# A routed-expert stage on one core: straight code per expert, transposes among the down products, up products as three rounded products

## The chip, the cores and the metric

The kernel runs on one core of one Trainium2 chip. The metric is the device time of one execution in microseconds. Three runs of the kernel before took 1823.43, 1825.82 and 1828.92 us; the median is 1825.82 us.

## The reference, cut to what matters

One inference step of a two-layer decoder trunk: 512 prompt tokens and 8 sample tokens, so T = 520 columns of D = 1024 channels, float32. Each layer has a mixer part and a feed-forward part; layer 0's is dense, layer 1's has eight routed experts of which each token uses two. Only the latter changes:

```python
def swiglu(h, w1, w3, w2):
    return (jax.nn.silu(h @ w1) * (h @ w3)) @ w2

def moe_swiglu(h, w_router, b_router, w1, w3, w2):
    logits = h @ w_router + b_router
    top_v, top_i = lax.top_k(logits, TOP_K)          # 2 of 8
    gates = jax.nn.softmax(top_v, axis=-1)
    comb = jnp.sum(one_hot(top_i, 8) * gates[..., None], axis=-2)
    y = jnp.zeros_like(h)
    for e in range(8):
        y = y + comb[..., e:e + 1] * swiglu(h, w1[e], w3[e], w2[e])   # 1024 -> 1408 -> 1024
    return y
```

## The kernel before, in words

All five engines run programs written out by hand and ordered by semaphores; nothing reorders them. After the router, GpSimd scatters each token's row of h to two places in a table in memory, `h_by_expert` (L695), so that the rows of an expert lie together. The counts of the eight experts sum to 1040. They are known only at run time: each engine reads them from the tile `count` (`tokens_of`, L325).

Then TensorE runs a loop over the eight experts (L1080 to L1087). For an expert with at most NW = 256 tokens (all eight here):

- `narrow_rows` (L981): two tiles of 128 rows from `stage` are transposed, 16 transposes of 128 by 128 (L988), into PSUM, and copied by VectorE (L1660) and ScalarE (L1308) into `hn`.
- `narrow_products` (L991), first loop, the **up products**: for each of ET = 11 blocks f of 128 hidden channels, w1 and w3 by `hn`, KD = 8 products of 128 by 128 by n each (L1006), 11 x 2 x 8 = 176 for one expert. They are plain float32 products, and the profile shows each as two pairs of a weight load (LDWEIGHTS) and a MATMUL, 352 pairs. ScalarE takes the Silu (L1313), VectorE the product (L1666) into `Gn`.
- its second loop, the **down products**: 8 blocks q of 11 products of w2 by `Gn` (L1019), 88 for one expert, plain float32, 176 pairs in the profile. ScalarE copies each block out (L1316); behind block q the two transposes of block q - 1 (L1028) turn it back to token rows, which VectorE copies (L1671) and SP's queue writes to `y_by_expert` (L501).

The number of columns n is a constant of the code, so there is one body of code for each of ten widths (`WIDTHS`: 128, 136, 144, 152, 160, 176, 192, 208, 224, 256). `narrow_by_width` (L1071) picks the body by nested comparisons, one for each width (L1076):

```python
                with pe.If(c <= widths[0]):
                    narrow_products(e, widths[0])
                with pe.Else():
                    narrow_by_width(e, c, widths[1:])
```

The forms of the matmuls show the widths that this input takes: expert 0 to 7 run at 128, 136, 128, 144, 136, 208, 152, 128 columns. For more than 256 tokens there is a body `wide`, not run here. SP's queue loads the weights in twelve chunks an expert into a ring of six slots (L525 waits for a slot), each chunk free again when the products that read it are done.

Elsewhere the kernel computes products in another form, which the change takes up. In layer 0's dense part and in both mixers a product of float32 tiles is made of three products of tiles of the rounded type float32r: the upper part of each operand is made by a rounding copy on ScalarE (L1132, L1148), the lower part by a subtraction on GpSimd or VectorE (L604, L1381), and TensorE sums upper by upper, upper by lower and lower by upper (L747 at 260 columns with weights 128 columns wide; L792 at 256 columns has only two of them, with a stationary tile 18 columns wide). In the profile each of these is one pair.

Of the kernel before, what the change touches and what calls it, by code (L numbers as in the profile page):

```python
# [38 lines left out]
AT = [0, 128, 256, 384, T - P]  # L49
PICKS = 2 * T  # L50
ROOM = PICKS + T
NW = 2 * P
WIDTHS = [128, 136, 144, 152, 160, 176, 192, 208, 224, NW]
# [46 lines left out]
def trunk_program(nc, A, O):  # L100
    ctx = ExitStack()
    with ctx:
# [93 lines left out]
        countf = sb("countf", [P, NE])  # L196
        count = sb("count", [P, NE], I32)
# [20 lines left out]
        hexp = cut(big, 11 * T, KD, T)  # L218
        hact = cut(big, 19 * T, 2, T)

        Gn = cut(big, 0, ET, NW)
        hn = cut(big, 11 * T, KD, NW)
        hactn = cut(big, 19 * T, 2, NW)
# [9 lines left out]
        lgT = stat2[0:NE]  # L233

# [62 lines left out]
        def norm_step(tag, k, n):  # L297
# [5 lines left out]
                                          "zero", "h_tr", "h_row", "in_tr", "in_ev", "in_ev1",  # L303
                                          "f_done", "f_act", "f_free", "y_done", "y_free", "yt_tr", "yt_ev",
                                          "y_out", "count", "exp_d", "diag", "g_mm", "g_ev", "x_tr", "x_ev",
                                          "ya", "ss", "ssr", "rr", "scaled", "mods", "const"]}
        Rout = [sem(f"moe_rows_out{t}") for t in range(NT)]
        Rwide = [sem(f"moe_wide_in{t}") for t in range(2, NT)]
# [21 lines left out]

        w_in_v = [A["w_in"][l].rearrange("(k p) (b n) -> b p k n", p=P, n=256) for l in range(DEPTH)]
# [6 lines left out]
        def expert_chunk(e, j):  # L338

            if j < 8:  # L340
                w = A["w1_moe" if j % 2 == 0 else "w3_moe"][0]
                n = P * min(3, ET - 3 * (j // 2))
                return w[e].rearrange("(k p) n -> p k n", p=P)[:, :, (j // 2) * 384:(j // 2) * 384 + n], KD, n
            return A["w2_moe"][0][e].rearrange("(k p) n -> p k n", p=P)[:, :, (j - 8) * 256:(j - 7) * 256], ET, 256

# [46 lines left out]
        def _(sp):  # L392
# [81 lines left out]
            def first_rows(row):  # L474
# [4 lines left out]
            def rest_of_rows(e):  # L479
                c, row = tokens_of(sp, e), first_of(sp, e)  # L480
                with sp.If(c <= NW):
                    for t in range(2, NT):
                        sp.sem_inc(Rwide[t - 2], 16)
                with sp.Else():
                    for t in range(2, NT):
                        free = sp.snap(sp.to_reg(NT * e + t - 1))
                        sp.wait_ge(const_ready, 1)
                        sp.wait_ge(R["in_tr"], free)
                        sp.dma_start(stage[:, t % 2, :], Hd[bass.ds(row + AT[t], P), :]).then_inc(Rwide[t - 2], 16)

            def rows_out(e):


                c, row = tokens_of(sp, e), first_of(sp, e)
                with sp.If(c <= NW):
                    sp.sem_inc(R["y_out"], 16 * (NT - 2))
                    for t in range(2):
                        there = sp.snap(sp.to_reg(NT * e + NT + t))
                        sp.wait_ge(const_ready, 1)
                        sp.wait_ge(R["yt_ev"], there)  # L500
                        sp.dma_start(Yd[bass.ds(row + P * t, P), :], yrow[:, t, :]).then_inc(R["y_out"], 16)  # L501
                with sp.Else():
                    for t in range(NT):
                        there = sp.snap(sp.to_reg(NT * e + t + 2))
                        sp.wait_ge(const_ready, 1)
                        sp.wait_ge(R["yt_ev"], there)
                        sp.dma_start(Yd[bass.ds(row + AT[t], P), :], stage[:, 2, :]).then_inc(R["y_out"], 16)

            sp.wait_ge(R["count"], 2)
            row0 = first_of(sp, 0)  # L510
            for t in range(NT):
                sp.wait_ge(Rout[t], 32)
            first_rows(row0)
            with sp.Fori(0, NE - 1) as e:
                rest_of_rows(e)
                row = first_of(sp, e + 1)
                free = sp.snap(sp.to_reg(NT * e + NT))
                sp.wait_ge(const_ready, 1)
                sp.wait_ge(R["in_tr"], free)
                first_rows(row)  # L520
                for j in range(PER_E):
                    which, n = used(e, j)
                    n = sp.snap(sp.to_reg(n))
                    sp.wait_ge(const_ready, 1)
                    sp.wait_ge(which, n)  # L525
                    j += EXPERT_RING
                    eload(j, expert_chunk(e, j) if j < PER_E else expert_chunk(e + 1, j - PER_E))
                rows_out(e)
            last = sp.snap(sp.to_reg(NE - 1))
            rest_of_rows(last)  # L530
            for j in range(PER_E - EXPERT_RING):
                sp.wait_ge(*used(NE - 1, j))
                eload(j + EXPERT_RING, expert_chunk(NE - 1, j + EXPERT_RING))
            rows_out(last)
# [18 lines left out]
        def _(pool):  # L553
# [67 lines left out]
            for l in range(DEPTH):  # L621
# [53 lines left out]
                if l == 0:  # L675
# [5 lines left out]
                    link(pool.memset(stage[0:T // 5, 2, :], 0.0))  # L681
                    pool.dma_start(Hd[PICKS:ROOM].rearrange("(a p) n -> p a n", a=5),
                                   stage[0:T // 5, 2:3, :].to_broadcast([T // 5, 5, D])).then_inc(R["zero"], 16)
# [1053 lines left out]
```

## Time and profile before

| what | us |
|---|---|
| median of the three runs | 1825.82 |
| span of the profiled execution, first to last instruction | 1826.2 |
| start of the first row transposes of expert 0 | 1076.21 |
| last transposes of expert 7 end | about 1783.2 |
| the stretch of the experts between these | 707.0 |
| TensorE matmuls busy in the whole span | 1479.6 |

The page gives no time of the profiled execution other than its span. An engine's busy time is the union of its instructions' durations. A MATMUL's duration (275 ns and more) is its latency, of which most overlaps its neighbours; how fast matmuls follow each other is read from the chain of waits, where a run of xN matmuls stands with the time in which it passed. "issue" is time in which an engine waited for nothing that the profile shows; the sequencer's own rows (here PEldq) say what it did in it.

### The profile page before, as it was taken

Reading aid. Unit: us, or ns where it says so; the run is one execution under the profiler, and the core shown is the slowest. Engines: PE = TensorE matmul, PEld = TensorE weight load, DVE = VectorE, ACT = ScalarE, POOL = GpSimd, SP = SyncE. Lnnn points to the kernel's source line nnn. Section 1 sums busy time; section 2 is a strip of 40 time slices with the busy share of each in tenths; the row PEclk is TensorE's granted clock in tenths of the full one; section 3 lists DMA queues with packets and bytes.
Section 4 is the critical chain, followed back from the end, with each engine's and each line's share of the span. In section 5 each row is a group of like instructions: output and inputs, shape, how many; then the busy total and the mean of one; then the engine's idle time right before and its main releaser. Section 6 shows DMA issues by size and latency. Waiting matters only on the chain.

```text
span 1826.2 us, 27269 instructions
## 1 busy us (share of the span) xinstructions
PE 1479.6 (81%) x11320; PEld 1411.8 (77%) x11321; DVE 602.4 (33%) x815; ACT 480.2 (26%) x662; POOL 397.8 (22%) x288
## 2 busy tenths in 40 slices
PE   5776877789999999989588859879796919949792
PEld 4555876679999999979577649869796919949692
DVE  6667697623112011146965320101101000000115
ACT  6677312422221122223133221111111100011114
POOL 1102560534434343434524020000000000000004
PEclk9998898899999999989899979889898959979896
DMA  9999121024333322322210469686685833637554
GB/s 321 300 337 316 48 91 46 28 70 120 93 87 98 105 93 56 96 93 70 69 47 6 164 218 306 209 295 210 241 269 183 300 109 110 216 104 234 173 171 163
DMA packets 249862, 286.02 MB, mean 157 GB/s; under 512 B 7589, under 2 KB 241719, under 8 KB 249686
## 3 DMA queue, kind: packets, MB, share of 16 engines
q1 hardware_dynamic: 244886, 272.17, 45.9%
q0 software_dynamic: 3632, 11.08, 1.8%
q8 instruction: 126, 2.06, 0.5%
q10 hardware_dynamic: 1200, 0.56, 0.1%
q14 instruction: 18, 0.15, 0.0%
HBM read 266.45 MB, written 18.05 MB: 156 GB/s over the span
## 4 chain that ended last, share of the span: by engine, by line
PE 66%; DVE 15%; issue 9%; DMA 5%; SPq 2%; ACT 1%; POOL 1%; POOLq 0%; ACTq 0%; DVEq 0%
PE PP L747 28%; PE PP L1006 20%; PE PP L1019 10%; DVE work L1477 7%; DMA mem<-in_w_ada 4%; PE PP L760 2%; DVE stat L1573 1%; PE PP L988 1%; PE PP L792 1%; PE PP L721 1%; PE PP L732 1%; SPq L424 1%; PE PP L1028 1%; DVE stat L1406 1%; DVE mem L1419 1%
## 5 line engine op out<-in xcount | busy, mean ns | idle before, releaser
L747 PE MATMUL PP<-hT_r,mem_r 128*128 128x260 f32 x2624 | 428.5, 284 | 4.6 <-DVE xT L1431 3.2
L1006 PE MATMUL PP<-big,mem 128*128 128x128 f32 (+4 forms) x2816 | 362.4, 293 | 49.5 <-issue 49.2
L1006 PEld LDWEIGHTS PP<-big,mem 128*128 128x128 f32 x2816 | 360.6, 195 | 52.1 <-issue 49.6
L604 POOL TENSOR_TENSOR mem_r<-mem,mem_r 128x1024 fp32r<-128x1024 f32 (+1 forms) x108 | 279.0, 2597 | 407.5 <-ACT mem_r L1132 406.9
L747 PEld LDWEIGHTS PP<-hT_r,mem_r 128*128 128x128 f32 x2624 | 362.4, 188 | 6.4 <-issue 2.5
L747 PE MATMUL PP<-mem_r 128*128 128x260 f32 x1312 | 263.8, 283 | 0.0
L747 PEld LDWEIGHTS PP<-mem_r 128*128 128x128 f32 x1312 | 201.7, 188 | 0.0
L1019 PE MATMUL PP<-big,mem 128*128 128x128 f32 (+4 forms) x1408 | 184.2, 288 | 0.0
L1019 PEld LDWEIGHTS PP<-big,mem 128*128 128x128 f32 x1408 | 178.1, 191 | 0.0
L703 POOL DMA_INDIRECT mem<-y_by_expert,place x10 | 9.6, 956 | 720.7 <-DMA y_by_expert<-work 717.9
L1666 DVE TENSOR_TENSOR big<-PP,big 128x256 f32<-128x256 f32 x88 | 37.4, 425 | 381.3 <-ACT big L1313 381.3
L1132 ACT ACTIVATE mem_r<-mem 128x1024 fp32r<-128x1024 f32 (+1 forms) x108 | 115.9, 1099 | 118.3 <-DMA mem<-in_w_dense 71.0
L747 PE MATMUL PP<-big_r,mem_r 128*128 128x260 f32 x1056 | 129.4, 284 | 2.9 <-DVE big L1592 2.9
L747 PEld LDWEIGHTS PP<-big_r,mem_r 128*128 128x128 f32 x1056 | 127.7, 188 | 3.6 <-DVE big L1592 3.3
L1313 ACT ACTIVATE big<-PP 128x256 f32<-128x256 f32 x88 | 33.8, 384 | 365.8 <-PE PP L1006 365.8
L1477 DVE SCALAR_TENSOR_TENSOR work<-big,vec,work 128x512 f32<-128x512 f32 x120 | 127.1, 1135 | 0.0
L1381 DVE TENSOR_TENSOR mem_r<-mem,mem_r 128x2048 fp32r<-128x2048 f32 x48 | 110.0, 2292 | 45.5 <-ACT mem_r L1148 45.5
L792 PE MATMUL PP<-mem_r,cs_r 128*18 128x256 f32 x768 | 103.6, 295 | 19.3 <-DVE mem_r L1381 18.4
L792 PEld LDWEIGHTS PP<-mem_r,cs_r 128*18 128x18 f32 x768 | 76.9, 102 | 43.7 <-DVE mem_r L1381 23.4
L988 PE MATMUL PP<-ident,stage 128*128 128x128 f32 x128 | 27.0, 399 | 96.6 <-issue 75.4
L988 PEld LDWEIGHTS PP<-ident,stage 128*128 128x128 f32 x128 | 24.3, 214 | 98.6 <-issue 77.0
L1148 ACT ACTIVATE mem_r<-mem 128x2048 fp32r<-128x2048 f32 x48 | 91.7, 1911 | 25.1 <-DMA mem<-in_w_ada 24.9
(239 smaller groups left out, 1155.1 us busy)
## 6 DMA issues: line engine op xcount, KB each, us to landing
mem<-in_w_moe SPq DMA_DIRECT2D x48, 1536.0 KB, 9.8
mem<-in_w_ada SPq DMA_DIRECT2D x48, 1024.0 KB, 11.2
mem<-in_w_moe SPq DMA_DIRECT2D x32, 1408.0 KB, 8.8
mem<-in_w_dense SPq DMA_DIRECT2D x20, 1024.0 KB, 5.6
mem<-in_w_in SPq DMA_DIRECT2D x16, 1024.0 KB, 5.5
mem<-in_w_moe SPq DMA_DIRECT2D x16, 1024.0 KB, 7.0
mem<-in_w_dense SPq DMA_DIRECT2D x16, 704.0 KB, 4.9
mem<-in_w_out SPq DMA_DIRECT2D x8, 1024.0 KB, 5.1
```

The lines of the kernel that those rows point to most:

```text
L604: pool.tensor_tensor(r_(raw), raw, read_(hi), ALU.subtract).then_inc(w_lo, 1)
L747: mm = pe.matmul(PP[q][:, h, 0:HT], r_(w[:, k, :]), r_(x[:, k, HT * h:HT * h + HT]), start=(i == 0 and w is wh and x is hi), stop=(i == le ...
L760: mm = pe.matmul(PP[q + c][:, h, 0:HT], r_(w[:, k, :]), r_(x[:, k, HT * h:HT * h + HT]), start=(i == 0 and w is wh and x is hi), stop=(i = ...
L792: mm = pe.matmul(PP[0][0:2 * NQ, j % 2, 0:256], r_(cs[:, k, :]), r_(w[:, k, :]), start=(k == 0 and not lower), stop=(k == KD - 1 and bool( ...
L988: tr = pe.transpose(PP[t][:, h, (j % 4) * P:(j % 4) * P + P], stage[:, t, j * P:(j + 1) * P], ident[:])
L1006: mm = pe.matmul(PP[w][:, f % 2, 0:n], expert_slot(2 * c + w, KD, m)[:, k, P * (f % 3):P * (f % 3) + P], hn[:, k, 0:n], start=(k == 0), st ...
L1019: mm = pe.matmul(PP[2][:, q % 2, 0:n], expert_slot(8 + q // 2, ET, 256)[:, k, P * (q % 2):P * (q % 2) + P], Gn[:, k, 0:n], start=(k == 0), ...
L1132: act.activation(r_(hi), raw, ACT.Copy).then_inc(w_hi, 1)
L1148: act.activation(r_(ahi[:, j % 3]), ada_slot(j), ACT.Copy).then_inc(ada_hi, 1)
L1381: dve.tensor_tensor(r_(ada_slot(j)), ada_slot(j), read_(ahi[:, j % 3]), ALU.subtract).then_inc(ada_lo, 1)
L1477: dve.scalar_tensor_tensor(acc, gin[:, ct, k:k + SEQ], tap("conv_c_w", k, ct), acc, ALU.mult, ALU.add).then_inc(s["conv_tap"], 1)
L1666: dve.tensor_tensor(Gn[:, f, :], PP[1][:, f % 2, 0:NW], hactn[:, f % 2, :], ALU.mult).then_inc(R["f_free"], 1)
```

## The change

- The loop over experts is written out eight times for TensorE, ScalarE, VectorE and SP. TensorE reads all counts once, ahead of the first expert. The widths are now 144, 160, 176, 208 and 256; a comparison `pe.br_lt` stands ahead of each body, and falls through into it if the count fits, else jumps over it to the next. A body closes with a jump to the next expert (`expert_over{e}`), for which a prefetch hint is set behind block q = 3 of the down products. With this input the bodies taken are 144 for six experts, 160 for expert 6 and 208 for expert 5.
- The row transposes of expert e + 1 stand behind blocks q = 3 and q = 5 of the down products of expert e (`rows_tr`), the transposes of y's last block behind f = 1 of the next expert (`y_tr`).
- The up products become three products of rounded tiles. ScalarE copies 128 by 2 by 8 by 128 weights (one block f of w1 and w3) to an upper tile (`upper_pair`), VectorE subtracts to leave the lower part in the ring slot (`lower_pair`), AHEAD = 3 blocks ahead of the products, over PAIRS = 4 tiles. `hn` becomes `hn_hi` and `hn_lo` (`rows_hi`, `rows_lo`). The down products stay as they are.
- The case of more than 256 tokens becomes one loop behind the straight code, entered if the largest count is over 256 (not the case here). POOL waits for one semaphore `y_all` that SP gives when all rows of y have landed. The zeroed end of `h_by_expert` grows from 520 to 768 rows.

```diff
-WIDTHS = [128, 136, 144, 152, 160, 176, 192, 208, 224, NW]
+WINDOWS = (T + NW - 1) // NW
+ROOM = PICKS + WINDOWS * NW
+WIDTHS = [144, 160, 176, 208, NW]
+AHEAD = 3
+PAIRS = 4
...
+            def expert(e, n, c):
                 for f in range(ET):
...
+                    if f == 0:
+                        pe.wait_ge(R["hn_lo"], 4 * e + 4)
+                    if ET * e + f >= 2:
+                        pe.wait_ge(R["f_free"], ET * e + f - 1)
+                    pe.wait_ge(R["pair_lo"], ET * e + f + 1)
+                    hi, lo = pair_hi(e, f), pair_raw(e, f)
                     for w in range(2):
                         for k in range(KD):
...
-                            mm = pe.matmul(PP[w][:, f % 2, 0:n], expert_slot(2 * c + w, KD, m)[:, k, P * (f % 3):P * (f % 3) + P],
-                                           hn[:, k, 0:n], start=(k == 0), stop=(k == KD - 1))
+                            for i, (wt, x) in enumerate(((hi, hn_hi), (hi, hn_lo), (lo, hn_hi))):
+                                mm = pe.matmul(PP[w][:, f % 2, 0:n], r_(wt[:, w, k, :]), r_(x[:, k, 0:n]),
+                                               start=(k == 0 and i == 0), stop=(k == KD - 1 and i == 2))
...
+                    if q:
+                        y_tr(e, q - 1)
+                    if q in (3, 5) and e + 1 < NE:
+                        rows_tr(e + 1, (q - 3) // 2)
+                    if q == 3 and n < NW:
+                        over = pe.mark_branch_hint_location()
+                if n < NW:
+                    pe.br_lt(c, T + 1, on_true=f"expert_over{e}", on_false=f"expert_over{e}").branch_hint(over)
...
+            def by_width(e, c, widths):
...
+                pe.br_lt(c, n + 1, on_true=here, on_false=f"expert{e}_over_{n}")
...
+            counts = [tokens_of(pe, e) for e in range(NE + 1)]
+            for t in range(2):
+                rows_tr(0, t)
+            for e in range(NE):
+                by_width(e, counts[e], WIDTHS)
+                nc.switch_bb(f"expert_over{e}")
+            y_tr(NE - 1, KD - 1)
...
+            def lower_pair(e, f):
+                raw = pair_raw(e, f)
+                dve.wait_ge(R["pair_hi"], ET * e + f + 1)
+                dve.tensor_tensor(r_(raw), raw, read_(pair_hi(e, f)), ALU.subtract).then_inc(R["pair_lo"], 1)
...
             for t in range(NT):
                 dve.wait_ge(Rout[t], 32)
...
+            for f in range(AHEAD):
+                lower_pair(0, f)
+            for t in range(2):
+                rows_lo(0, t)
+            for e in range(NE):
...
+                if e + 1 < NE:
+                    rows_lo(e + 1, 0)
+                if e:
+                    dve.wait_ge(R["y_out"], 32 * e)
+                y_rows(e, 0)
+                if e + 1 < NE:
+                    rows_lo(e + 1, 1)
+                    for f in range(AHEAD):
+                        lower_pair(e + 1, f)
```

How the instructions of TensorE stand at the start of the experts' code, before: the head of the loop (L1082), the reading of the count, the row transposes, the first comparison and the first products of the 128-column body.

```order
L1082 UNCONDITIONAL_BRANCH
L1082 ISA
L325 TENSOR_LOAD count
L325 ISA x2
L1084 COMPARE_AND_BRANCH
L985 ISA
L988 MATMUL PP<-ident,stage 128x128 x16
L1076 COMPARE_AND_BRANCH
L979 ISA
```

The same place with the change, from the reading of the last count: `big_r` holds the upper weights and both parts of the rows, `mem_r` the lower weights in their slot.

```order
L328 TENSOR_LOAD count
L328 ISA x2
L995 MATMUL PP<-ident,stage 128x128 x16
L1055 COMPARE_AND_BRANCH
L1022 MATMUL PP<-big_r 128x144 x2
L1022 MATMUL PP<-big_r,mem_r 128x144
```

The loop, its reading and its outer comparison are gone from each expert, and a plain product has become three rounded ones.

TensorE at the end of one body, before (the 128-column one), from block q = 6 of the down products on:

```order
L1019 MATMUL PP<-big,mem 128x128 x11
L1024 REGISTER_ALU
L1028 MATMUL PP<-ident,work 128x128 x2
L1019 MATMUL PP<-big,mem 128x128 x11
L1024 REGISTER_ALU
L1028 MATMUL PP<-ident,work 128x128 x2
L1024 REGISTER_ALU
L1028 MATMUL PP<-ident,work 128x128 x2
L1076 UNCONDITIONAL_BRANCH
```

With the change (the 144-column body), from block q = 3 on:

```order
L1035 MATMUL PP<-big,mem 128x144 x11
L1006 MATMUL PP<-ident,work 128x128 x2
L995 MATMUL PP<-ident,stage 128x128 x8
L1043 BRANCH_PREFETCH_HINT
L1035 MATMUL PP<-big,mem 128x144 x11
L1006 MATMUL PP<-ident,work 128x128 x2
L1035 MATMUL PP<-big,mem 128x144 x11
L1006 MATMUL PP<-ident,work 128x128 x2
L995 MATMUL PP<-ident,stage 128x128 x8
L1035 MATMUL PP<-big,mem 128x144 x11
```

The sixteen row transposes (L995, before L988) have moved from the head of an expert into the down products of the one before it, eight at a time.

VectorE with the change, from the last blocks of one expert to the first of the next: L1726 is the product after Silu, L1710 the lower part of the rows, L1717 the copy of y's rows, L1703 the subtraction of a pair of weight blocks.

```order
L1726 TENSOR_TENSOR big<-PP,stat 128x256 x3
L1710 TENSOR_TENSOR big_r<-PP,big_r 128x4x128 x2
L1717 COPY work<-PP 128x512 x2
L1710 TENSOR_TENSOR big_r<-PP,big_r 128x4x128 x2
L1703 TENSOR_TENSOR mem_r<-mem,hT_r 128x16x128 x2
L1703 TENSOR_TENSOR mem_r<-mem,big_r 128x16x128
L1726 TENSOR_TENSOR big<-PP,stat 128x256
```

Three subtractions of weights now stand on VectorE between the rows of the next expert and its first product.

## Rows read from the trace of the kernel before

**Rows 1.** The page: span, and TensorE's busy time in the span.

```profile
span 1826.2 us, 27269 instructions
PE 1479.6 (81%) x11320; PEld 1411.8 (77%) x11321; DVE 602.4 (33%) x815; ACT 480.2 (26%) x662; POOL 397.8 (22%) x288
```

**Rows 2.** Groups by line, 1076 to 1784 us: busy us, mean ns | idle before.

```profile
L1006 PE MATMUL PP<-big,mem 128*128 128x128 f32 (+4 forms) x2816 | 362.4, 293 | 49.5 <-issue 49.2 <-DVE big L1660 0.3
L1019 PE MATMUL PP<-big,mem 128*128 128x128 f32 (+4 forms) x1408 | 184.2, 288 | 0.0
L988 PE MATMUL PP<-ident,stage 128*128 128x128 f32 x128 | 27.0, 399 | 96.6 <-issue 75.4 <-DMA stage<-h_by_expert 21.3
```

**Rows 3.** Chain of waits in order of time: start us, us, what.

```profile
1072.94 3.23 DMA stage<-h_by_expert
1076.21 3.67 PE PP L988 x16
1079.88 39.61 PE PP L1006 x352
...
1124.41 0.22 PE PP L1028 x2
1124.62 2.46 PE PP L1019 x22
...
1361.48 2.70 PE PP L1019 x22
...
1462.70 13.11 issue
...
1479.47 26.30 issue
...
1578.03 3.87 PE PP L1019 x22
...
1685.71 2.85 PE PP L1019 x22
```

**Rows 4.** TensorE's sequencer at the comparisons of line L1076, 1479 to 1506 us: ns min/median/max.

```profile
L1076 PEldq COMPARE_BRANCH  x8: 81/4837/5203, 1475.9 to 1505.2; - x8
```

**Rows 5.** Durations of weight loads and matmuls by line: ns min/median/max.

```profile
L1006 PEld LDWEIGHTS PP<-big,mem x2816: 186/190/338, 1079.8 to 1760.9; 128*128 128x128 f32 x188
L747 PEld LDWEIGHTS PP<-hT_r,mem_r x2624: 186/188/193, 203.5 to 1028.0; 128*128 128x128 f32 x188
L792 PEld LDWEIGHTS PP<-mem_r,cs_r x768: 93/96/152, 11.7 to 174.1; 128*18 128x18 f32 x192
L792 PE MATMUL PP<-mem_r,cs_r x768: 275/278/418, 11.7 to 174.3; 128*18 128x256 f32 x192
```

**Rows 6.** Rounded products in a row: the chain at L747, the timeline at L792.

```profile
1009.35 5.76 PE PP L747 x48
...
105.37 2.02 PE L792 MATMUL PP<-mem_r,cs_r 128*18 128x256 f32 x16 [0.99 <-DVE mem_r L1381]
```

**Rows 7.** Groups of ScalarE and VectorE by line: the splitting, and the experts' copies.

```profile
L1381 DVE TENSOR_TENSOR mem_r<-mem,mem_r 128x2048 fp32r<-128x2048 f32 x48 | 110.0, 2292 | 45.5 <-ACT mem_r L1148 45.5
L1671 DVE COPY work<-PP 128x512 f32<-128x512 f32 x32 | 20.6, 687 | 175.8 <-PE PP L1028 175.8
L1666 DVE TENSOR_TENSOR big<-PP,big 128x256 f32<-128x256 f32 x88 | 37.4, 425 | 381.3 <-ACT big L1313 381.3
L1148 ACT ACTIVATE mem_r<-mem 128x2048 fp32r<-128x2048 f32 x48 | 91.7, 1911 | 25.1 <-DMA mem<-in_w_ada 24.9
L1313 ACT ACTIVATE big<-PP 128x256 f32<-128x256 f32 x88 | 33.8, 384 | 365.8 <-PE PP L1006 365.8
L1308 ACT ACTIVATE big<-PP 128x512 f32<-128x512 f32 x16 | 9.6, 598 | 86.3 <-PE PP L988 86.3
```

**Rows 8.** The experts' stretch: PE, PEld, DVE, ACT, POOL busy, clock, DMA share, GB/s.

```profile
1076.20:1783.20 707.00, 580.00 (x4480) 573.41 (x4480) 67.83 (x135) 87.19 (x183) 0.00 (x0) 0.90 0.62 205
```

**Rows 9.** The page's DMA issues: an expert's first weight chunks, us to landing.

```profile
mem<-in_w_moe SPq DMA_DIRECT2D x48, 1536.0 KB, 9.8
```

More of the change, by code:

```diff
@@ L472, in used, with rows_in @@
                 return R["y_done"], KD * e + 2 * (j - 8) + 2
-            def first_rows(row):
+            def rows_in(row):
                 for t in range(2):
                     sp.dma_start(stage[:, t, :], Hd[bass.ds(row + P * t, P), :]).then_inc(Rin[t], 16)
[L479 to L507, printed above, removed]
+            def rows_out(e, row):
+                for t in range(2):
+                    sp.wait_ge(R["yt_ev"], 4 * e + 3 + t)
+                    sp.dma_start(Yd[bass.ds(row + P * t, P), :], yrow[:, t, :]).then_inc(R["y_out"], 16)
@@ L509, in _ @@
             sp.wait_ge(R["count"], 2)
-            row0 = first_of(sp, 0)
+            row = first_of(sp, 0)
             for t in range(NT):
                 sp.wait_ge(Rout[t], 32)
[L513 to L520, printed above, removed]
-                for j in range(PER_E):
[L522 to L534, printed above, removed]
+            rows_in(row)
+            for e in range(NE):
+                before_row = row
+                for j in range(PER_E):
+                    if e + 1 < NE or j + EXPERT_RING < PER_E:
+                        sp.wait_ge(*used(e, j))
+                        eload(j, expert_chunk(e, j + EXPERT_RING) if j + EXPERT_RING < PER_E else
+                              expert_chunk(e + 1, j + EXPERT_RING - PER_E))
+                    if j == 1 and e:
+                        rows_out(e - 1, last_row)
+                    if j == 1 and e + 1 < NE:
+                        row = first_of(sp, e + 1)
+                        sp.wait_ge(R["in_tr"], 2 * e + 2)
+                        rows_in(row)
+                last_row = before_row
@@ L536, in _ @@
+            sp.wait_ge(R["y_out"], 32 * NE)
+            sp.sem_inc(R["y_all"], 1)
             for t in range(NT):
@@ L1071, in narrow_by_width @@
-            def narrow_by_width(e, c, widths):
+                    if KD * e + q >= 2:
+                        pe.wait_ge(R["y_free"], KD * e + q - 1)
+                    for k in range(ET):
+                        if q == 0 and k in (0, ET - 1):
+                            pe.wait_ge(R["f_free"], ET * e + (ET - 1 if k == 0 else ET))
+                        mm = pe.matmul(PP[2][:, q % 2, 0:n], expert_slot(PER_E * e + 8 + q // 2, ET, 256)[:, k, P * (q % 2):P * (q % 2) + P],
+                                       Gn[:, k, 0:n], start=(k == 0), stop=(k == ET - 1))
@@ L1090, in _ @@
-            pe.wait_ge(R["f_free"], ET * NE + 2)
+                pe.br_lt(c, n + 1, on_true=here, on_false=f"expert{e}_over_{n}")
+                with nc.body(here, valid_engines=[pe.engine]):
+                    expert(e, n, c)
+                with nc.body(f"expert{e}_over_{n}", valid_engines=[pe.engine]):
+                    by_width(e, c, widths[1:])
+            pe.wait_ge(R["count"], 2)
+            counts = [tokens_of(pe, e) for e in range(NE + 1)]
+            for t in range(2):
+                rows_tr(0, t)
@@ L1091, in _ @@
+            pe.wait_ge(R["f_free"], ET * NE)
             pe.wait_ge(R["diag"], 1)
@@ new lines, in _ @@
+            with act.If(tokens_of(act, NE) > NW):
+                with act.Fori(0, NE) as e:
+                    for w in range(WINDOWS):
+                        x = e * WINDOWS + (NE + w)
+                        for f in range(ET):
+                            act.wait_ge(R["f_done"], reg(act, ET * x + f + 1))
+                            act.wait_ge(R["f_free"], reg(act, ET * x + f))
+                            act.activation(hactn[:, f % 2, :], PP[0][:, f % 2, 0:NW], ACT.Silu).then_inc(R["f_act"], 1)
+                        act.wait_ge(R["yt_tr"], reg(act, 2 * x))
+                        for q in range(KD):
+                            act.wait_ge(R["y_done"], reg(act, KD * x + q + 1))
+                            act.activation(yn[:, q, :], PP[2][:, q % 2, 0:NW], ACT.Copy).then_inc(R["y_free"], 1)
+                act.nop()
```

358 lines of the change are left out of this document (191 added, 167 removed).

## The prediction

> **What bounds the kernel now.** I read the page first: TensorE is busy 1479.6 of 1826.2 us, no other engine over a third [rows 1]. Then the groups of the experts' stretch: of its 707.0 us (1076.2 to 1783.2) the up products take 362.4, the down products 184.2, the row transposes 27.0, and TensorE stands idle 75.4 + 49.2 = 124.6 us for "issue", that is, for nothing another engine does [rows 2]. The rest is the transposes of y. (Its clock is 0.90 in the mean [rows 8].) So two things decide this stretch: how fast TensorE takes its products, and the time in which it has no instruction. ScalarE and VectorE wait for TensorE there 366 and 381 us [rows 7], so they have room. The idle time is the sequencer's: a comparison that leads out of the code at hand takes about 4.8 us, where the quick ones take 0.08 [rows 4]; expert 5, at the eighth of ten widths, waits 13.11 us before its row transposes and 26.30 more before its first product [rows 3].
>
> **Up products, the largest term.** Before: 352 pairs of weight load and matmul for an expert. After: 11 x 2 x 8 x 3 = 528 pairs, 4224 for eight experts. What does one cost at 144 columns? A plain pair at 128, 144, 152 and 208 columns takes 2.46, 2.70, 2.85 and 3.87 us for 22, which is 112, 123, 129 and 176 ns [rows 3]. From 144 to 208 this is a straight line, 0.83 ns a column (two cycles of 2.4 GHz a column), and it would give 109 at 128. The row there is 112: something other than the columns holds it. That is the weight load: it takes 190 ns for 128 columns in a plain pair, 188 in a rounded one, and 96 for 18 columns [rows 5]. 92 ns for 110 columns are 0.84 ns a column, 107 ns for 128, and a few ns more to change over make 112. Since a rounded tile's load lasts as long as a plain one's, and every rounded matmul has a load of its own (the page counts 11321 loads for 11320 matmuls, [rows 1]), I price a rounded pair at **112 ns at any width up to 208**: 4224 x 0.112 = 473.1 us, against 362.4, **+110.7**.
>
> No rounded product of fewer than 256 columns is in the trace, so this price has bounds. Above: what it takes at 260 columns, 5.76 us for 48 = 120 ns [rows 6]; that is more than the 108 of its columns, and 16 of them with 18-column weights at 256 columns pass, without the last one's duration, in (2.02 - 0.28) / 15 = 116 [rows 5, 6], so a rounded matmul may carry some 8 ns that a plain one doesn't. Below: its columns alone, 120/260 = 0.46 ns each, 67 ns at 144, if the loads cost nothing. I take 112 because the row at 128 plain columns is nearest: same load, same stage.
>
> The Trainium skill, on the page "TensorE: Matmul & The Clock Gate", section "LDWEIGHTS", gives columns / 1.2 ns for a weight load, 107 ns for 128; the section on weight-path perf modes adds that the fast load brings nothing for fp32. By that figure alone the term would be an estimate of 4224 x 107 = 452 us and the total 21 us lower. It speaks against this change: three loads take the place of two.
>
> **Idle time.** Six experts fall through into the 144 body, with no jump. Expert 6 (160) jumps once over a body, expert 5 (208) three times: 4 x 4.9 = 20 us, less some 4 us that work in TensorE's queue covers (before, too, its transposes covered 3.7 of the jumps at expert 5), plus 3 us for products at the lower clock behind the two stalls: 19. The closing jumps I take as free, since the hint stands some 13 us ahead of each. -124.6 + 19 = **-105.6**.
>
> **Widths.** Down products of three experts go from 128 to 144 (8 x (2.70 - 2.46) = 1.9 us each), two from 136 to 144 (8 columns on that line are 6.6 ns, times 176 pairs 1.2 each), one from 152 to 160 (22 pairs 2.85 to 2.99 by the line, 1.2): **+9.4**. The other two stay.
>
> **Row transposes.** Now 27.0 us [rows 2], since 16 take 3.67 us [rows 3] at the start of each expert, 229 ns each, at the lower clock behind the stall. Among the down products they go at 0.22 us for two [rows 3]: 128 x 0.11 = 14, and 2 more for those of expert 0, which stay where they are: **-11**. They must not hold the queue: rows arrive early (their load goes out at the third block f) and q = 3 comes long after.
>
> **Splitting.** A pair of blocks is 2048 elements on each partition: 1.91 us on ScalarE, 2.29 on VectorE [rows 7]. For one f, VectorE has 2.29 + 0.43 = 2.7 us and ScalarE 1.91 + 0.38 = 2.3, against 48 x 0.112 = 5.4 of TensorE: hidden. If TensorE's block took under 2.7 us they would be the bound.
>
> At the boundary it is tight. A down block with its transposes takes 2.9 us. Behind q = 5 (at 18 us, 19 with eight row transposes) ScalarE has two copies of 0.60 and an upper pair of 1.91, to about 22; VectorE then subtracts for 2.29, to 24.0. TensorE ends block 7 at 24.5. The second and third pair are due 5.4 us apart and ready in time. I charge 0.5 us a boundary, **+3.5**; the bounds are 0 and 7 x 2.3 = 16 if the first pair is late by a whole subtraction.
>
> **Start.** VectorE's first three subtractions stand behind its wait for the scattered rows, over by 1072.9 [rows 3]: with four lower parts of rows at 0.69, 3 x 2.29 + 4 x 0.69 = 9.6 [rows 7], so the first product starts at 1082.5 instead of 1079.9: +2.6. TensorE idles meanwhile, and the clock may be low a little longer: +2. Together **+4.6**.
>
> **End.** One semaphore more, and SP jumps over the unused loop before it gives it: the jump (up to 4.9) runs beside the write of y's last rows: **+1.5**.
>
> **Weights** are no bound: the stretch stays about as long as it was, and its mean transfer share was 0.62 [rows 8]. The first chunks of the next expert go out at the end of the up products and land in 9.8 us [rows 9], before q = 5 asks for them.
>
> **Sum:** 110.7 - 105.6 + 9.4 - 11 + 3.5 + 4.6 + 1.5 = +13.1. The profiled execution's span of 1826.2 lies 0.4 above the median, so 1825.8 + 13.1 = **1839 us**. Two large changes nearly cancel. A change under 0.3% (5.5 us) can't be told from none here.
>
> **Rivals.**
> 1. *The loads don't bound.* If the load of a 128-column rounded tile is hidden behind something that lets two overlap, a pair costs its columns: 67 ns at 144, 74 at 160, 96 at 208. The up products then take 528 x (6 x 0.067 + 0.074 + 0.096) = 302 us, 171 less: **1668 us**, much faster than before. From what pair price on does the sign turn? 473.1 - 13.1 = 460, or 109 ns a pair. For it: no rounded row below 256 columns. Against it: 112 instead of 109 at 128 columns, and equal load durations in both forms. Chance 0.14. The same page of the Trainium skill, section "Back-to-back issue gap", has about 81 ns a pair sustained at 128 columns; by that the estimate would be 4224 x 81 = 342 us of up products, 131 less than mine, 1708 us. No run here shows it, and its loads are not said to be of fp32.
> 2. *The rounded matmul's extra stays.* A pair costs 120 ns as in the dense part: 507 us, +34, **1873 us**. For it: 116 even with short loads. Against: the columns leave 40 ns of room now. Chance 0.1.
> 3. *The hint does nothing.* Seven closing jumps at 4.8 us each, partly covered: +30, **1869 us**. For it: every far branch before cost that [rows 4], and none had a hint. Chance 0.09.
> 4. *Rounded products under 256 columns run no faster than plain ones*, that is, two plain pairs each: 245 ns at 144, 272 at 160, 352 at 208: 528 x (6 x 0.245 + 0.272 + 0.352) = 1106 us, **about 2470**. Nothing in the trace speaks for it but the missing row. Chance 0.05.
>
> **Numbers.** The forecast has 0.62, in 1816 to 1852 (all jumps hidden and no boundary loss below; 1 to 2 ns a pair or late first pairs above); of it 0.07 falls under 1820.3, 0.16 within 0.3%, 0.39 above. With the rivals: faster 0.07 + 0.14 = 0.21; same 0.16; slower 0.39 + 0.24 = 0.63. The range of 1815 to 1878 takes in the forecast and rivals 2 and 3, 0.81; rivals 1 and 4 stay out.
>
> **What would show it.** Right: the chain shows 48 rounded matmuls of one f in 5.4 us at every width, an expert's 528 in about 59 us; TensorE idle by "issue" about 20 us, at experts 5 and 6 alone; granted clock 1.0 through the other experts; weight loads at 188 ns. Wrong: 48 in 3.2 us (rival 1), in 5.8 (rival 2) or 11.8 (rival 4); seven gaps of 4 to 5 us at the ends of experts (rival 3); TensorE waiting for VectorE's subtraction at the first product of each expert for more than a microsecond.

## The result, and the profile after

The changed kernel takes 2056.6 us in the median of four runs (2055.41 to 2056.81), the kernel before, on the same chip, 1827.0: a ratio of 1.126, with a 95% interval of 1.1244 to 1.1276. Forecast were 1839 us and at most 1878. It is 230 us slower, and 217 of them were not in the sum.

The head of the page after: the span, TensorE's busy time, and the granted clock in 40 slices, in tenths of full speed.

```profile
span 2053.6 us, 29105 instructions
PE 1810.9 (88%) x12728; PEld 1746.3 (85%) x12728; DVE 812.2 (40%) x919; ACT 626.5 (31%) x750; POOL 397.7 (19%) x288
...
PEclk9998988999999999988975575575699989855996
```

TensorE is busier than in [rows 1], not idler, and the clock line has what no line of before had: slices of 0.5 while TensorE is busy all through (the one slice of 0.5 before is the jump ahead of expert 5, with TensorE nearly idle). The chain of waits shows the experts one after the other (start us, us, what); L1022 is the rounded up product, L1035 the down product, L995 the row transposes:

```profile
1083.05 111.78 PE PP L1022 x528
1194.84 6.54 PE PP L1035 x44
...
1222.93 19.51 PE PP L1022 x96
1242.43 0.43 PE PP L1006 x2
1242.87 92.07 PE PP L1022 x432
...
1382.43 92.07 PE PP L1022 x432
...
1500.61 10.68 PE PP L1022 x96
1511.29 0.24 PE PP L1006 x2
1511.53 48.20 PE PP L1022 x432
...
1595.53 48.20 PE PP L1022 x432
...
1697.18 48.23 PE PP L1022 x432
...
1805.06 92.08 PE PP L1022 x432
...
1936.81 48.20 PE PP L1022 x432
```

There are two prices and nothing between: 48.20 / 432 = 111.6 ns a pair at experts 3, 4, 5 and 7, which is the 112 of the forecast, and 92.07 / 432 = 213 ns at experts 0, 1, 2 and 6. The windows of up products of experts 1, 3 and 6 (PE, PEld, DVE, ACT, POOL busy, clock, DMA share, GB/s) say why:

```profile
1222.90:1334.90 112.00, 111.97 (x531) 112.00 (x532) 26.07 (x21) 18.22 (x18) 0.00 (x0) 0.51 0.30 102
...
1500.60:1559.70 59.10, 59.10 (x532) 59.10 (x531) 27.70 (x22) 20.26 (x20) 0.00 (x0) 1.00 0.60 196
...
1784.00:1897.10 113.10, 113.10 (x531) 113.10 (x532) 23.79 (x20) 18.22 (x18) 0.00 (x0) 0.50 0.28 94
```

The clock is 0.50 to 0.51, that is 1.2 GHz, for a whole block of up products, with no idle time in it, and 1.00 (2.4 GHz) in another with the same instructions. Where the clock fell can be read at expert 1: the first 1.4 us of its products pass at full clock, the rest at half, and the down products behind them are back at 0.96.

```profile
1222.90:1224.30 1.40, 1.37 (x12) 1.40 (x13) 1.40 (x1) 0.00 (x0) 0.00 (x0) 0.99 1.03 384
1224.30:1334.90 110.60, 110.60 (x521) 110.60 (x521) 24.67 (x21) 18.22 (x18) 0.00 (x0) 0.50 0.30 99
1334.90:1361.50 26.60, 25.97 (x207) 25.73 (x206) 7.81 (x9) 9.54 (x16) 0.00 (x0) 0.96 0.87 297
```

The up products of the eight experts take 111.8 + 111.6 + 111.4 + 58.9 + 58.9 + 61.4 + 112.7 + 58.9 = 685.6 us, against 473.1 in the forecast: 212.5 of the missing 217. What TensorE waits for in the experts' stretch (us in total, times, longest):

```profile
PE PP L1022 <- issue: 15.1, 1, 15.1
PE PP L1022 <- DVE mem_r L1703: 8.2, 3, 4.3
...
PE PP L1022 <- DVE big_r L1710: 2.2, 1, 2.2
```

25.5 us, where [rows 2] had 124.6. The three waits put down to VectorE are not VectorE's at all: they stand at experts 1, 2 and 6, where the sequencer's rows show it still in a branch. These are the closing branches of experts 0 and 1 and of all experts (ns min/median/max):

```profile
L1045 PEldq COMPARE_BRANCH  x1: 4111/4111/4111, 1218.5 to 1218.5; - x1
L1045 PEldq COMPARE_BRANCH  x1: 3839/3839/3839, 1358.5 to 1358.5; - x1
...
L1045 PEldq COMPARE_BRANCH  x8: 316/770/4111, 1218.5 to 2005.8; - x8
```

The hint worked at most experts (five of the other six take 0.3 to 1.2 us, expert 5's 2.4) and not at experts 0 and 1, which leaves TensorE 2.1 us without a product ahead of expert 1 and 1.8 ahead of expert 2. Expert 6 has its expected jump over a body (4.3 us without a product), expert 5 its three (15.1), expert 0 the wait for the first split pairs.

So there is a pattern: the four experts at half clock all begin behind a gap, and of those that begin without one none is. The exception is expert 5, behind the longest gap, but at 208 columns: its first block pair is slow (13.20 us for 96, not 10.7) and then the clock is back.

### The profile page after: what moved, and what is told of

It reads as the page before. It is cut to its first block, busy times and chain, and to the rows that moved or that the text cites. A ratio compares the mean times of both kernels' runs of the same rounds, so it can differ in the third digit from the quotient of the medians.

```text
span 2053.6 us, 29105 instructions
## 1 busy us (share of the span) xinstructions
PE 1810.9 (88%) x12728; PEld 1746.3 (85%) x12728; DVE 812.2 (40%) x919; ACT 626.5 (31%) x750; POOL 397.7 (19%) x288
## 4 chain that ended last, share of the span: by engine, by line
PE 75%; DVE 14%; DMA 4%; issue 3%; ACT 2%; SPq 2%; POOL 1%; POOLq 0%; DVEq 0%; ACTq 0%
PE PP L1022 33%; PE PP L756 25%; PE PP L1035 9%; DVE work L1525 6%; DMA mem<-in_w_ada 4%; PE PP L769 2%; PE PP L801 2%; DVE stat L1621 1%; PE PP L730 1%; PE PP L741 1%; DVE mem_r L1703 1%; DVE stat L1454 1%; PE PP L1006 1%; DVE mem L1467 1%; DVE mem_r L1463 1%
## 5 line engine op out<-in xcount | busy, mean ns | idle before, releaser
L1022 PE MATMUL PP<-big_r,mem_r 128*128 128x144 f32 (+2 forms) x1408 | 485.1, 345 | 0.0
L1022 PEld LDWEIGHTS PP<-big_r,mem_r 128*128 128x128 f32 x1408 | 369.0, 262 | 0.0
L1022 PE MATMUL PP<-big_r,hT_r 128*128 128x144 f32 (+2 forms) x1408 | 339.6, 345 | 23.4 <-issue 15.1
L1022 PE MATMUL PP<-big_r 128*128 128x144 f32 (+2 forms) x1408 | 339.0, 344 | 2.2 <-DVE big_r L1710 2.2
L1022 PEld LDWEIGHTS PP<-big_r,hT_r 128*128 128x128 f32 x1408 | 298.7, 262 | 24.2 <-issue 24.2
L1022 PEld LDWEIGHTS PP<-big_r 128*128 128x128 f32 x1408 | 298.2, 262 | 2.6 <-DVE big_r L1710 2.6
L1035 PE MATMUL PP<-big,mem 128*128 128x144 f32 (+2 forms) x1408 | 198.9, 299 | 0.0
L1726 DVE TENSOR_TENSOR big<-PP,stat 128x256 f32<-128x256 f32 x88 | 37.4, 425 | 407.3 <-ACT stat L1346 407.3
L1035 PEld LDWEIGHTS PP<-big,mem 128*128 128x128 f32 x1408 | 191.7, 195 | 0.0
L756 PEld LDWEIGHTS PP<-big_r,mem_r 128*128 128x128 f32 x1056 | 127.7, 188 | 3.6 <-DVE big L1640 3.3
L1703 DVE TENSOR_TENSOR mem_r<-mem,big_r 128x2048 fp32r<-128x2048 f32 x44 | 100.7, 2293 | 65.0 <-ACT big_r L1324 50.1
```

Source lines behind the costliest of these rows:

```text
L756: mm = pe.matmul(PP[q][:, h, 0:HT], r_(w[:, k, :]), r_(x[:, k, HT * h:HT * h + HT]), start=(i == 0 and w is wh and x is hi), stop=(i == le ...
L1022: mm = pe.matmul(PP[w][:, f % 2, 0:n], r_(wt[:, w, k, :]), r_(x[:, k, 0:n]), start=(k == 0 and i == 0), stop=(k == KD - 1 and i == 2))
L1035: mm = pe.matmul(PP[2][:, q % 2, 0:n], expert_slot(PER_E * e + 8 + q // 2, ET, 256)[:, k, P * (q % 2):P * (q % 2) + P], Gn[:, k, 0:n], sta ...
L1703: dve.tensor_tensor(r_(raw), raw, read_(pair_hi(e, f)), ALU.subtract).then_inc(R["pair_lo"], 1)
L1726: dve.tensor_tensor(Gn[:, f, :], PP[1][:, f % 2, 0:NW], hactn[:, f % 2, :], ALU.mult).then_inc(R["f_free"], 1)
```

## The experiments

**Theory A.** A rounded pair at 144 or 160 columns takes 112 ns because of its weight load, and columns stream in about half of that. In such a stretch the granted clock stays at the level it has: high if the expert follows the down products without a gap, low if a gap came first. **Theory B.** The 213 ns are a cost of place or traffic (experts 1, 2, 5 and 6 keep their first pair in another tile than experts 3, 4 and 7; expert 0, slow as well, keeps it in the tile of those three). **Theory C.** A rounded pair's price goes by its columns.

### More columns in the same products

```diff
-mm = pe.matmul(PP[w][:, f % 2, 0:n], r_(wt[:, w, k, :]), r_(x[:, k, 0:n]),
+mm = pe.matmul(PP[w][:, f % 2, 0:max(n, 240)], r_(wt[:, w, k, :]), r_(x[:, k, 0:max(n, 240)]),
```

> The kernel after, but the up products always run over at least 240 columns (the further columns are other experts' rows, whose results nobody uses); nothing else changes. Theory A (the clock: while a rounded pair takes 112 ns for its weight load and only 60 of them carry columns, the granted clock stays at the level at which the expert began, and the experts that begin behind a gap stay at 1.2 GHz): with 240 columns in the same 112 ns the clock comes back within some microseconds in every expert, each expert's up products take 59 to 62 us, and the time falls by 4 x 53 = 211 us to about 1845. Theory B (the 213 ns of experts 0, 1, 2 and 6 are a cost of the place: memory traffic, or the tile in which the pair lies): no change, 2055. Theory C (a rounded pair's price goes by its columns): slower everywhere.

Measured: 1846.64 us, 1.0126 of the kernel before (1.0109 to 1.0143). Its chain and its window at expert 1:

```profile
1183.59 48.38 PE PP L1022 x432
```

```profile
1172.40:1232.00 59.60, 59.60 (x532) 59.60 (x533) 26.08 (x21) 18.28 (x18) 0.00 (x0) 1.00 0.57 192
```

With two thirds more columns in each product the kernel is 210 us faster. 48.38 / 432 = 112.0 ns at 240 columns against 111.6 at 144: in this range the price does not go by the columns, theory C is out, and the weight load as the bound stands. The gaps are still there (its closing branches of experts 0 and 1 take 4.0 and 3.8 us), the tiles and the addresses are the same, and the clock is 1.00: theory B is out too. Behind these two gaps (2.0 and 1.8 us) the clock did not fall at all, unlike in the kernel after. That it also comes back once it has fallen is seen at expert 6, behind a gap of 4.8 us:

```profile
1626.54 13.53 PE PP L1022 x96
...
1640.29 48.38 PE PP L1022 x432
```

The first 96 pairs take 13.53 us, not 10.8, at a mean clock of 0.80, the rest pass at 1.00. The 1847 us lie 8 from the forecast of 1839.

### Plain up products in the new order

```diff
-                            for i, (wt, x) in enumerate(((hi, hn_hi), (hi, hn_lo), (lo, hn_hi))):
-                                mm = pe.matmul(PP[w][:, f % 2, 0:n], r_(wt[:, w, k, :]), r_(x[:, k, 0:n]),
-                                               start=(k == 0 and i == 0), stop=(k == KD - 1 and i == 2))
+                            mm = pe.matmul(PP[w][:, f % 2, 0:n], raw[:, w, k, :], hn_hi[:, k, 0:n],
+                                           start=(k == 0), stop=(k == KD - 1))
...
-                    if f + AHEAD < ET:
-                        upper_pair(e, f + AHEAD)
...
-                dve.wait_ge(R["pair_hi"], ET * e + f + 1)
-                dve.tensor_tensor(r_(raw), raw, read_(pair_hi(e, f)), ALU.subtract).then_inc(R["pair_lo"], 1)
```

TensorE waits for the weight chunks themselves, and VectorE copies the rows.

> The kernel after with the up products as plain float32 products again (no splitting of weights or rows; VectorE copies the rows), everything else as it is: straight code, widths, moved transposes. Theory A: plain pairs at 144, 160 and 208 columns take 123, 136 and 176 ns and the clock stays up; up products 6 x 43 + 48 + 62 = 368 us instead of 688, start 9 us earlier: 2054 - 320 - 9, about 1725, that is some 100 under the kernel before. Rival: the slow clock comes from the new order (transposes among the down products, gaps at the closing branches), not from the rounded products; then experts 0, 1, 2 and 6 stay slow here too, and the time is 1725 + 4 x 40 = 1885.

Measured: 1733.73 us, 0.9503 of the kernel before (0.9487 to 0.9519). **This kernel beats both**, by 91 and by 323 us. Its groups between 1076 and 1690 us, against [rows 2]:

```profile
L1023 PE MATMUL PP<-big,mem 128*128 128x144 f32 (+2 forms) x2816 | 372.9, 295 | 23.3 <-issue 22.0 <-DVE big L1699 1.4
...
L1036 PE MATMUL PP<-big,mem 128*128 128x144 f32 (+2 forms) x1408 | 193.5, 294 | 0.0
```

372.9 us of up products (362.4 before, at finer widths), 193.5 of down products (184.2), and 23.3 us idle instead of 124.6. The chain at expert 1 has no gap and no slow stretch (in this code the closing branches of experts 0 to 3 all take 0.3 us, so that this run does not say by itself what plain products do behind a short gap; the kernel without hints, below, does):

```profile
1150.95 0.22 PE PP L1006 x2
1151.17 7.84 PE PP L1023 x64
1159.02 0.22 PE PP L1006 x2
1159.23 35.28 PE PP L1023 x288
```

A plain pair at 144 columns takes 35.28 / 288 = 122.5 ns; two make 245, three rounded ones 336. The straight code and the moved transposes are the gain of this change, and the rounded products the whole loss: 323 us of 2057. Some 210 of these are the clock, which the 240 columns gave back, and the 113 between 1846.64 and 1733.73 are what the rounded products cost at full clock.

### A gap where there was none

```diff
-                    pe.wait_ge(R["pair_lo"], ET * e + f + 1)
+                    pe.wait_ge(R["pair_lo"], ET * e + f + (3 if f == 0 and e in (3, 4, 7) else 1))
```

> The kernel after, but TensorE begins experts 3, 4 and 7 only when VectorE has subtracted three pairs of weights, not one, which puts a gap of some 4 to 5 us there, where there was none. Theory A: their up products drop to 1.2 GHz as well and stay there, 112 us instead of 59: 2054 + 3 x (53 + 4.5) = 2226. Theory B (place, tile or traffic decides, not the gap): the gaps alone, 2054 + 14 = 2068.

Measured: 2235.27 us (one run; beside it 1824.88 for the kernel before), 179 above the kernel after. Experts 3 and 7 in the chain, and the window of expert 3:

```profile
1526.39 92.07 PE PP L1022 x432
...
2070.30 92.07 PE PP L1022 x432
```

```profile
1505.20:1618.40 113.20, 113.16 (x531) 113.19 (x532) 23.79 (x20) 18.23 (x18) 0.00 (x0) 0.50 0.28 93
```

All three fell to 1.2 GHz and stayed there. Three waits of 4.5 us cost 179 us. Their products, tiles and slots are unchanged, so at these three it is the gap that decides.

### Dense products ahead of the slow experts

```diff
+                    if f == 0 and e in (0, 1, 2, 6):
+                        for _ in range(36):
+                            pe.matmul(PP[0][:, 1, 0:P], ones[:], ident[:], start=True, stop=True)
```

> The kernel after with 36 plain products of 128 x 128 (72 pairs, 8 us at full clock, their results overwritten) ahead of the first up product of experts 0, 1, 2 and 6, the four that ran at 1.2 GHz. Theory A: the clock is up when the rounded products begin and stays up through the expert, so the four give back 53 us each for 8 to 14 us of filler: about 1880. If the clock falls during rounded products at 144 columns whatever it was before, no gain: 2054 + 32 = 2086.

Measured: 1872.65 us (one run). The four experts with useless products ahead of them now pass as fast as the others; experts 0 and 1:

```profile
1094.80:1153.70 58.90, 58.90 (x529) 58.90 (x529) 22.60 (x18) 18.27 (x18) 0.00 (x0) 1.00 0.47 153
1186.60:1245.70 59.10, 59.10 (x532) 59.10 (x531) 23.78 (x20) 18.24 (x18) 0.00 (x0) 1.00 0.51 170
```

The same rounded products at 144 columns hold 2.4 GHz for 59 us if they find it. Together with the run before: both levels last through an expert's 528 products.

But the run is a test of the filler at two experts only. What TensorE waits for ahead of the useless products (L1020; us in total, times, longest):

```profile
PE PP L1020 <- issue: 5.0, 2, 2.8
PE PP L1020 <- DVE big_r L1713: 2.1, 1, 2.1
```

The 2.1 us are at expert 0, where the useless products (1084.9 to 1094.8 us, mean clock 0.83) begin behind the gap and have the clock back at 1.00 when the rounded ones begin. The 5.0 us are at expert 6, where the clock is 1.00 from the first useless product on. At experts 1 and 2 there is no gap any more: the longer code moved the late branches, and the closing branches of experts 0 and 1 take 0.37 and 0.33 us instead of 4.1 and 3.8. These two experts are fast for want of a gap, with or without filler, so that the hit near 1880 is in part luck.

### Two of the three rounded products

On the kernel with 240 columns, the product with the lower weights is left out of the sum; the splitting stays.

```diff
-for i, (wt, x) in enumerate(((hi, hn_hi), (hi, hn_lo), (lo, hn_hi))):
+for i, (wt, x) in enumerate(((hi, hn_hi), (hi, hn_lo))):
```

> The kernel with up products over 240 columns, with two of the three rounded products (the product of the lower weights is left out of the sum; the splitting stays). If every pair costs its weight load of 112 ns whatever it carries: 352 pairs take 39.4 us an expert instead of 59.1, 1846 - 8 x 19.7 = 1689, unless the splitting becomes the bound (a block f then takes 3.6 us against 2.7 on VectorE) or the first pairs of an expert come later than now. If the price lay in a wait for each block instead, less.

Measured: 1685.97 us (one run), 161 below 1846.64; expected were 8 x 19.7 = 158.

```profile
1156.43 32.26 PE PP L1022 x288
```

32.26 / 288 = 112.0 ns again. The cost is by the pair. VectorE and ScalarE keep up at 3.6 us a block too, with VectorE busy 21.1 of 32.3 us: within an expert the splitting is not the bound.

### The hint: earlier, and none

Earlier, on the kernel after: the hint behind block q = 0 instead of q = 3.

```diff
-                    if q == 3 and n < NW:
+                    if q == 0 and n < NW:
```

> The kernel after with the prefetch hint of the closing branch ahead of everything that follows block q = 0 of the down products, three blocks earlier. In the kernel after the closing branches of experts 0 and 1 still took 4.1 and 3.8 us on TensorE's sequencer and left 2.1 us without a product, where the others took 0.3 to 1.2 and left none. Theory A (the clock stays at the level at which a gap leaves it): if the earlier hint takes these gaps away, experts 1 and 2 keep 2.4 GHz and the time falls by 2 x 55 to about 1945; if the gaps stay, 2054. Theory D (the far branches depend on where the code lies, not on when the hint comes): the gaps stay, about 2054.

Measured: 2058.58 us (one run), no change. The closing branches of experts 0 and 1 still take 4.0 us:

```profile
L1045 PEldq COMPARE_BRANCH  x2: 3991/4005/4019, 1221.5 to 1361.4; - x2
```

Not the lead of the hint, then. In the kernels with the same number of instructions (up240, gap_at_3_4_7 and this one) the late branches stand at experts 0 and 1 as in the kernel after; where the code has another length they stand elsewhere (two_of_three: one of 3.8 us, at the end of expert 2; plain_up: one of 3.9, at expert 4; filler: none at experts 0 and 1), which fits theory D, that it depends on where the code lies. No run moves the code and nothing else, and the rule behind it stays open.

None, on the kernel with plain products:

```diff
-                    if q == 3 and n < NW:
-                        over = pe.mark_branch_hint_location()
...
-                    pe.br_lt(c, T + 1, on_true=f"expert_over{e}", on_false=f"expert_over{e}").branch_hint(over)
+                    pe.br_lt(c, T + 1, on_true=f"expert_over{e}", on_false=f"expert_over{e}")
```

> The kernel with plain up products in straight code, without the prefetch hints. Theory: each closing branch then is a far jump of 4 to 5 us, of which the queued products cover some 2: 6 or 7 such gaps of 2 to 4 us, 1733 + 15 to 30 = 1748 to 1763, the clock falling for some microseconds behind them at most. If the hints do nothing (rival 3 of the prediction): 1733.

Measured: 1768.18 us, 0.9676 of before (0.966 to 0.9693). The closing branches with and without a hint:

```profile
L1046 PEldq COMPARE_BRANCH  x8: 302/330/3915, 1148.9 to 1683.8; - x8
```

```profile
L1044 PEldq COMPARE_BRANCH  x8: 3301/3904/5422, 1150.1 to 1718.6; - x8
```

The hints are worth 34 us, somewhat more than expected; each missing one leaves 2.0 to 2.3 us without a product, and more where an open jump follows at once. Rival 3 of the prediction is refuted.

### Widths

On the kernel with plain products, the width 176 left out, and, in another kernel, 128 put in instead of 176:

```diff
-WIDTHS = [144, 160, 176, 208, NW]
+WIDTHS = [144, 160, 208, NW]
```

> The kernel with plain up products, with the widths 144, 160, 208 and 256 (176 left out). Expert 5 jumps twice instead of three times: 4.9 us less, nothing else changes for these counts: 1733 - 5 = 1728. If the far jumps depend on where the code lies, some closing branches change as well, by 2 us each either way.

Measured: 1733.33 us (0.9486, 0.9467 to 0.9505), the same as plain_up. Expert 5 does jump once less (its gap falls from 19.5 to 10.4 us, since there its closing branch is quick as well), but a closing branch of 4.1 us now stands at expert 2, and the two jumps left take 5.5 and 6.4 us. TensorE's waits for "issue" sum to 18.3 us, against 22.0; the expected 5 us did not show in the time.

```diff
-WIDTHS = [144, 160, 176, 208, NW]
+WIDTHS = [128, 144, 160, 208, NW]
```

> The kernel with plain up products, with the widths 128, 144, 160, 208 and 256. Three experts run at 128 without a jump and save 352 x 11 ns + 1.9 = 5.8 us each, 17 together; the five others jump once more, of which some 2 of 4.9 us are covered: +15. Expected 1733 - 2, about the same; if the first far jump of an expert stays covered (as the second width did in the kernel before), down to 1716.

Measured: 1748.75 us (0.9573, 0.9553 to 0.9594), 15 us slower than without the width: a miss. Its sequencer at the open comparisons behind expert 0, and what TensorE waits for:

```profile
L1056 PEldq COMPARE_BRANCH  x15: 70/4794/7534, 1142.7 to 1639.7; - x15
```

```profile
PE PP L1023 <- issue: 43.6, 7, 15.4
```

43.6 us of issue, against 18.3 without the width 128 and 22.0 in plain_up. The jump over one body behind expert 0 takes 6.5 us, not 4.9, and leaves 5.3 of them without a product, so the queue covers less of it than the 2 us I had put. The second width of the kernel before had cost nothing, with smaller bodies and sixteen transposes ahead of them; that did not carry over.

### The place of the row transposes

On the kernel with plain products, all sixteen behind the last block:

```diff
-                    if q in (3, 5) and e + 1 < NE:
-                        rows_tr(e + 1, (q - 3) // 2)
+                    if q == KD - 1 and e + 1 < NE:
+                        rows_tr(e + 1, 0)
+                        rows_tr(e + 1, 1)
```

> The kernel with plain up products, with all sixteen row transposes of the next expert behind the last down block instead of behind blocks 3 and 5. The transposes themselves cost TensorE the same 1.8 us; new is that the next up products wait for the copies of the second tile, 0.3 + 2 x 0.7 = 1.7 us, and for what stands ahead of them on VectorE: 7 x 1.7 to 2.5 = 12 to 18 us, 1733 + 15 = 1748, the clock staying up (plain products at 144 columns bring it back within microseconds if it falls). If the place of the transposes were worth nothing: 1733.

Measured: 1748.33 us (0.9573, 0.9553 to 0.9593), 14.6 above plain_up. The chain at the start of expert 1:

```profile
1152.75 0.02 issue
1152.78 2.50 DVE big L1700 x4
1155.27 0.04 issue
1155.32 8.11 PE PP L1023 x64
```

2.5 us of copies that little covers stand ahead of expert 1 and of most others; from the first product of expert 1 to that of expert 2 it is 70.16 us, against 68.20. But of the 14.6 us, some 2.4 are not the place: in the profiled executions the first product of expert 0 starts at 1085.38 instead of 1082.93, and ahead of it the two kernels do the same. The place among the down products is worth some 12 us, the low end of the 12 to 18 expected.

## Why the prediction was wrong

**The price of a rounded pair was right, the clock was missing.** The step that failed is "I price a rounded pair at 112 ns at any width up to 208: 4224 x 0.112 = 473.1 us": the up products took 685.6 us, because the granted clock was 0.5 through four of the eight experts, and the sum had nothing for that but 3 us behind the two stalls of experts 5 and 6 and 2 us at the start. At 2.4 GHz a pair takes 111.6 to 112.0 ns at 144 to 240 columns, all by its weight load, as worked out from the 112 ns of the plain pair at 128 columns. But I took 2.4 GHz as given, with only "3 us for products at the lower clock" behind the stalls. That holds for plain products, which bring the clock back within microseconds: in the kernel before behind each stall, and in plain_no_hint, where the first 64 pairs behind a gap of 2 us take 8.1 to 9.8 us instead of 7.8 and the next 288 their 35.28. Rounded products at 144 and 160 columns don't bring it back; those at 208 (expert 5) and 240 do. At 213 ns, half of the experts cost 53 us more each.

The rows to doubt it were there: I worked out myself that "the columns leave 40 ns of room", used it against rival 2, and did not ask what such products do to TensorE's clock. All rounded rows of before are at 256 and 260 columns, where by the prediction's own line the columns (108 ns at 260) take as long as the load. Rival 4, slower products below 256 columns, was the nearest in kind, but with 245 ns at every expert and for another reason. Why few columns fail to bring the clock back, and where between 160 and 208 columns that ends, no run here shows.

The Trainium skill, on the page "TensorE: Matmul & The Clock Gate", section "HAM oscillation — how this bites in real kernels", blames the low clock on idle gaps, waits for transfers, between bursts of matmuls, and advises to order the loops so that TensorE is not left waiting, or to pad the small dimension M. The trace agrees that a gap starts it (2.1 and 1.8 us at experts 1 and 2 were enough here). It disagrees that gaps are all: in these stretches TensorE has no idle time, PE busy 111.97 of 112.00 us, and stays at 1.2 GHz.

**The other terms, together, were right.** Without the rounded products the prediction's terms give -105.6 + 9.4 - 11, + 2 for a late clock at the start and + 1.5 for the end; plain up products at the coarser widths, which it had no term for, add 10.5 (372.9 against 362.4): -93. Measured, in plain_up: -91. In the kernel after itself, 685.6 - 473.1 = 212.5 us and a sum of 13.1 make 226, of 230.

- Idle time: 16 for the jumps (the 19 less its 3 for the lower clock), 3.5 at the boundaries and 2.6 at the start forecast, 25.5 found, but not placed as forecast. The three jumps of expert 5 left 15.1 us, the one of expert 6 4.3; "the closing jumps I take as free" failed at two of seven, by 2.1 and 1.8 us. In a sum they are nothing. At these two places they brought the low clock, and it cost 105 us.
- The boundary: the first split pair was ready 0.3 to 0.6 us before TensorE was free; the term of 3.5 us was none. The waits the profile puts down to VectorE there are the sequencer's.
- Row transposes: eight in 0.87 us at full clock, as forecast. Their place is worth some 12 us besides, since the copies behind them are hidden; the sum had no term of its own for that.
- Start: first product at 1083.05, forecast 1082.5. But the clock, once low there, cost 53 us and not 2.

**Rivals.** 1 is out (112 ns at 240 columns and 112 at 144, both by the load). 2 is out: the 8 ns more of the dense part don't show. 3 is out as a rule: the hints are worth 34 us. 4 is out: 112 ns at full clock, and 213, not 245, at half. The sign was right; the size was off by a factor of seventeen.

## What to carry to other kernels

Count what a product form costs by the pair of weight load and matmul, not by columns alone: a rounded pair cost 112 ns from 144 to 240 columns. Three rounded products beat one plain one (two pairs) only where the columns of the plain pairs take more than one and a half loads; worked out from these rows, at full clock and without the splitting, that is above some 200 columns (176 ns at 208, and 2 x 176 against 3 x 112). And don't assume that the clock comes back behind a stall: rounded products at 144 and 160 columns did not bring it back, while plain ones did, and rounded ones at 208 and 240 too, though these are bound by their weight loads as well. Look at the granted clock by stage, find the gap ahead of a low stretch, and add columns or density before shaving instructions.

## What the hardware showed that I had not expected

- Two stable speeds of the same instructions: 59 us and 112 us for 528 rounded pairs, kept from near its start to its end in all 28 stretches at 144 and 160 columns of four kernels (after and hint_at_q0 4 slow and 3 fast each, with added gaps 7 slow, with filler 7 fast), slow behind each gap of 1.8 us and more that stood directly ahead of the rounded products. At 208 and 240 columns the low level did not last.
- More work was faster: 240 columns instead of 144 took 210 us off, and the kernel with 8 us of useless products ahead of each of four experts was 184 us faster, though at two of these four the gap had gone with the moved branches.
- A hinted branch takes 0.3 us at most places, an unhinted closing one 3.3 to 5.4, and an open jump over bodies up to 7.5. But a hint fails at some places (3.8 to 4.2 us), the same two in four kernels with code of the same length, and moving the hint doesn't change it.
